# Attention of two token groups interleaved stage by stage, with the modulation vectors moved to other places

## The chip, the cores and the metric

The kernel runs on one core of one Trainium2 chip. The metric is the device time of one execution in microseconds (us). The kernel before was timed three times: 1448.36, 1448.42 and 1449.55 us, median 1448.42.

A core has engines that each work through their own list of instructions in order: PE (TensorE, matmuls into the PSUM banks), DVE (VectorE), ACT (ScalarE), POOL (GpSimd) and SP (SyncE, which here only issues DMAs). They wait for one another through semaphores. A DMA moves data from memory into the core while the engines work.

## The reference

Two layers of a transformer trunk, for two groups of 128 tokens with 1024 channels: context tokens (the prompt, group 0) and latent tokens (the sample, group 1). Per layer and group:

```python
h = adaln(rmsnorm(y, g_pre_mix[li]), m[0], m[1])        # m: six vectors per group
qa, ka, va, qb, kb, vb, up = split_projection(h @ w_in[li])     # 1024 -> 2560 columns
o_a = rmsnorm(diff_attention(qa, ka, va, lam), g_diff[li]) * (1.0 - lam_init)
o_b = dense_attention(qb, kb, vb)                       # sample: neighbourhood attention
o_c = multiscale_pool(up, pool_w[li], pool_scale[li])
y = y + m[2] * rmsnorm(merge_heads(o_a, o_b, o_c, w_out[li]), g_post_mix[li])
h = adaln(rmsnorm(y, g_pre_ffn[li]), m[3], m[4])
f = moe_ffn(h, ...)                                     # 64 experts, 8 per token, and a shared one
y = y + m[5] * rmsnorm(f, g_post_ffn[li])
```

The vectors are `m = silu(c) @ w_ada[li] + b_ada[li]`, cut into six of 1024; the prompt has its own `c`. Differential attention makes two softmaxes per head (four heads) and subtracts one, scaled by lambda, from the other. The sample's queries and keys are rotated first, and it also reads 128 cached context keys and values, so its scores have 256 columns where the prompt's have 128. All is fp32; the keys and values of the prompt are outputs too.

## The kernel before, in words

All is one program with the order written out by hand. Each layer has these stages.

*In-projection.* Tokens are normalised, transposed and modulated; the matrix `w_in` comes in five blocks of 512 columns. A projection is done as a split product (`split_product`, L651): activations and weights are cut into a high and a low part, and three products are added (high x high, low x high, high x low), 48 matmuls a block for both groups. The high part of a weight block is a copy by ACT (`high_weights`, L962), the low part a subtraction by DVE (`low_weights`, L1109). ACT copies the result of group 0, DVE that of group 1, into `U`. POOL rotates the sample's queries and keys (L482 to L487), after the last block.

*Attention.* `attention(l, 0)` runs whole, then `attention(l, 1)`: transposes of queries and keys (L535), scores (L546, or L549 and L550), exponentials on ACT (L984), combination of the two softmaxes on DVE (L1193), transposes of the weights (L585), values (L594), the same for the other heads (L564 to L610), and the pooling (L554, L579). The second call waits for the first to finish (`cat_done`), since both use the same buffers (`qkT`, `probs`, `wT`) and banks.

*Out-projection.* The concatenated heads are transposed (L515) and multiplied by `w_out` in two blocks; the vectors are spread over the partitions (L623).

*Experts.* Router, shared expert and the routed experts in pairs, in a loop. It takes most of the time, and the change does not touch it.

*Vectors.* The twelve vectors (six per layer, both groups at once) are made one at a time: `modulate` is 64 matmuls of 128x256 (L673) over two weight blocks, into a given PSUM bank, and `finish_vector` (L1122, L1126) adds the bias on DVE. If the bank was used for an earlier vector, PE first waits for that one's finish. Two vectors are made ahead of layer 0; in layer 0's attention five more (two of them in a row) and three in layer 1's; one behind each out-projection.

*Weight ring.* All weights ahead of the experts go through a ring of six blocks of 2 MB, in the order of the list from `blocks_before_experts`. SP issues block k when block k - 6 is done. An entry `("hi", ...)` is the place of a high part, which is not loaded; `("spare", k)` is an empty place. SP handles the list strictly in order, so a load whose place is not free holds up all behind it.

Line numbers here and in the rows are those of the kernel before.

## Time and profile before

| | |
|---|---|
| Three runs | 1448.36, 1448.42, 1449.55 us |
| The profiled execution | 1448.93 us, its span 1447.1 us |
| PE busy | 1357.5 us, 94% of the span |
| DVE, ACT, POOL busy | 466.7, 334.9, 60.3 us |
| Stages of layer 0 | in-projection 41.1 to 99.1, attention to 152.3, out-projection to 185.4 |
| Stages of layer 1 | in-projection 747.4 to 805.5, attention to 856.0, out-projection to 889.9 |

The span is what the profiler recorded of one execution, from its first to its last instruction. A busy PE is one with a matmul under way; its clock can still be at the lower of two levels (1.2 and 2.4 GHz), which the rows show as a granted clock of 0.50 against 1.00. The stages were cut by the first and last matmul of their kind.

### The profile page before, as it was taken

How to read it: one execution, taken by the hardware profiler on the slowest of the kernel's cores; microseconds unless marked ns; L12 is line 12 of the kernel's file. 1: busy time of each engine (PE TensorE's matmuls, PEld its weight loads, DVE VectorE, ACT ScalarE, POOL GpSimd, SP SyncE). 2: the span in 40 equal slices, each digit the busy share in tenths (PEclk: the TensorE clock that was granted, in tenths of full speed). 3: DMA queues.
4: the chain of work that ended last, by engine and by line, in shares of the span. 5: the costliest groups of instructions: out<-in, count | busy, mean ns of one | idle time of the engine just before them, and what ended most of it. 6: DMA issues, size and time to landing. Idle time of an engine off the chain costs nothing.

```text
span 1447.1 us, 30291 instructions
## 1 busy us (share of the span) xinstructions
PE 1357.5 (94%) x12298; PEld 744.4 (51%) x12298; DVE 466.7 (32%) x1110; ACT 334.9 (23%) x598; POOL 60.3 (4%) x89
## 2 busy tenths in 40 slices
PE   3898989999999999999969788999999999999996
PEld 2775744544544544544548575454454454454443
DVE  0625473222222222222264264622222222222223
ACT  1523441111111111111143344211111111111111
POOL 0120020000000000000020202000000000000000
PEclk8898989999999999999979978999999999999998
DMA  9789368999999999999656936399999999999990
GB/s 368 260 317 401 126 262 324 389 399 415 402 403 407 407 394 419 398 402 413 235 204 232 369 118 262 160 365 405 417 395 406 418 391 400 414 407 390 416 400 38
DMA packets 86294, 497.42 MB, mean 344 GB/s; under 512 B 7728, under 2 KB 7728, under 8 KB 36336
## 3 DMA queue, kind: packets, MB, share of 16 engines
q1 hardware_dynamic: 84416, 491.58, 84.7%
q0 software_dynamic: 1840, 5.31, 1.1%
q8 instruction: 27, 0.44, 0.1%
q14 instruction: 11, 0.09, 0.0%
HBM read 494.24 MB, written 2.62 MB: 343 GB/s over the span
## 4 chain that ended last, share of the span: by engine, by line
PE 88%; DVE 4%; ACT 3%; DMA 1%; issue 1%; SPq 1%; POOL 1%; POOLq 0%; ACTq 0%
PE PS L856 30%; PE PS L887 16%; PE PS L831 12%; PE PS L651 11%; PE PS L848 9%; PE PS L673 1%; PE PS L799 1%; DMA weights<-in_w_in 1%; PE PS L875 1%; PE PS L820 1%; SPq L384 1%; DVE h L1168 1%; PE PS L594 1%; PE PS L838 1%; ACT h L969 1%
## 5 line engine op out<-in xcount | busy, mean ns | idle before, releaser
L856 PE MATMUL PS<-weights,gathered 128*32 128x512 f32 (+1 forms) x3968 | 451.3, 592 | 0.0
L856 PEld LDWEIGHTS PS<-weights,gathered 128*32 128x32 f32 (+1 forms) x3968 | 133.6, 111 | 306.3 <-issue 306.3
L887 PE MATMUL PS<-weights,hiddenT 128*32 128x512 f32 (+1 forms) x1984 | 233.0, 595 | 0.0
L831 PEld LDWEIGHTS PS<-pick,x_parts 128*128 128x128 bf16 x3168 | 177.2, 98 | 54.7 <-issue 54.7
L831 PE MATMUL PS<-pick,x_parts 128*128 128x128 bf16 x3168 | 188.3, 219 | 0.0
L1473 DVE SCALAR_TENSOR_TENSOR hidden<-PS,slot_gate,silu 128x256 f32<-128x256 f32 x64 | 31.0, 484 | 397.8 <-ACT silu L1058 397.8
L1065 ACT ACTIVATE y_hi<-PS 128x512 fp32r<-128x512 f32 x128 | 76.4, 597 | 297.3 <-PE PS L887 297.3
L1483 DVE TENSOR_TENSOR y_lo<-PS,y_hi 128x512 fp32r<-128x512 f32 x128 | 88.5, 692 | 140.1 <-ACT y_hi L1065 140.1
L1058 ACT ACTIVATE silu<-PS 128x256 f32<-128x256 f32 x64 | 24.5, 383 | 417.5 <-PE PS L856 417.5
L887 PEld LDWEIGHTS PS<-weights,hiddenT 128*32 128x32 f32 (+1 forms) x1984 | 60.5, 110 | 116.0 <-issue 114.6
L651 PE MATMUL PS<-weights_split,hT_high 128*128 128x512 f32 x448 | 112.3, 407 | 7.8 <-ACT hT_high L943 6.0
L651 PEld LDWEIGHTS PS<-weights_split,hT_high 128*128 128x128 f32 x448 | 86.9, 196 | 30.4 <-issue 11.5
L848 PE MATMUL PS<-y_hi,put 128*128 128x512 f32 x264 | 88.4, 416 | 2.9 <-DVE y_lo L1483 2.9
L848 PE MATMUL PS<-y_lo,put 128*128 128x512 f32 x264 | 82.8, 395 | 0.0
L1476 DVE COPY gathered<-PS 128x512 f32<-128x512 f32 x64 | 44.3, 692 | 118.9 <-PE PS L831 118.9
L1109 DVE TENSOR_TENSOR weights_split<-weights,weights_split 128x4096 fp32r<-128x4096 f32 x14 | 61.6, 4421 | 9.8 <-ACT weights_split L962 9.8
L1439 DVE CAST put<-PS 128x256 fp32r<-128x256 bf16 x66 | 28.0, 424 | 103.9 <-PE PS L840 103.9
L437 POOL TENSOR_SCALAR rstd<-sum_squares 128x1 f32<-128x1 f32 x16 | 8.4, 528 | 1165.4 <-ACT h L969 1157.5
L673 PE MATMUL PS<-weights,c_columns 128*32 128x256 f32 x768 | 47.0, 399 | 9.5 <-DMA weights<-in_w_ada 9.5
L848 PEld LDWEIGHTS PS<-y_lo,put 128*128 128x128 f32 x264 | 49.5, 188 | 11.9
L651 PE MATMUL PS<-weights_split,hT_low 128*128 128x512 f32 x224 | 54.5, 395 | 0.0
L1060 ACT ACTIVATE gathered<-PS 128x512 f32<-128x512 f32 x64 | 38.2, 597 | 66.2 <-PE PS L831 66.2
(250 smaller groups left out, 983.5 us busy)
## 6 DMA issues: line engine op xcount, KB each, us to landing
weights<-in_w_gate SPq DMA_DIRECT2D x128, 1024.0 KB, 7.6
weights<-in_w_up SPq DMA_DIRECT2D x128, 1024.0 KB, 11.6
weights<-in_w_down SPq DMA_DIRECT2D x128, 1024.0 KB, 9.0
weights<-in_w_ada SPq DMA_DIRECT2D x24, 2048.0 KB, 13.1
weights<-in_w_in SPq DMA_DIRECT2D x9, 2048.0 KB, 8.3
weights<-in_w_out SPq DMA_DIRECT2D x4, 2048.0 KB, 15.9
weights<-in_w_in SPq DMA_DIRECT2D x2, 1024.0 KB, 24.1
weights<-in_ws_gate SPq DMA_DIRECT2D x2, 1024.0 KB, 5.1
```

What stands on the lines that cost most here:

```text
L651: last = mm(PS[:, banks[g], :], rows_[:, j, g, :], w[:, j * HALF:(j + 1) * HALF], start=start and j == 0, stop=w is lo and j == KT - 1, sk ...
L673: last = mm(PS[32 * q:32 * q + 32, bank, 0:QUARTER], cb[:, jj, :, :].rearrange("p g c -> p (g c)"), w[:, j, q * QUARTER:(q + 1) * QUARTER] ...
L831: last = mm(PS[:, 5 + half, j * P:(j + 1) * P], x3[:, g, part, jj, :], pick[:, u % 2, g, 0:P], start=(g, part) == (0, 0), stop=(g, part) = ...
L848: last = mm(PS[:, 2 * g + n, :], put[:, u % 2, g * T:(g + 1) * T], y[:, n * HALF:(n + 1) * HALF], start=False, stop=False, skip_group_chec ...
L856: last = mm(PS[a:z, 4, :].rearrange("p (a n) -> p a n", a=2), xgT[:, b, j, a:z], w[:, e, :, j, :], start=j == 0, stop=j == KT - 1, tile_po ...
L887: last = mm(PS[a:z, bank, :], hidT[:, j, a:z], w[:, e, j, n * HALF:(n + 1) * HALF], start=j == 0, stop=j == FT - 1, tile_position=(0, a), ...
L1060: run(*gathered(1 - b, 0), ACT.Copy).then_inc(S["xg_a"], 1)
L1065: run(yhi[:, n * HALF:(n + 1) * HALF], PS[:, bank, :], ACT.Copy).then_inc(S["yhi_done"], 1)
L1109: v.tensor_tensor(lo, w, hi.bitcast(f32), ALU.subtract).then_inc(w_low, 1)
L1473: v.scalar_tensor_tensor(hid[:, :], PS[:, 4, F:2 * F], slot_gate[:, b:b + 1], silu[:, :], ALU.mult, ALU.mult)\
L1476: v.tensor_copy(xgT[:, 1 - b, 4:8, :], PS[:, 6, :].rearrange("p (j s) -> p j s", j=4)).then_inc(S["xg_d"], 1)
L1483: v.tensor_tensor(ylo[:, cols], PS[:, bank, :], yhi[:, cols].bitcast(f32), ALU.subtract).then_inc(S["ylo_done"], 1)
```

## The change

Both groups now go through attention together: `attention(l)` on PE, ACT and DVE alternates between the groups, stage by stage. To that end each group has its own buffers (`qkT`, probabilities, transposed weights, pooled rows, row sums and maxima), laid over memory that is not in use at the time, and its own PSUM banks. The cache transposes go ahead of the last in-projection block, and POOL's rotation may start after the second block (its scratch is `h` and no longer `probs`). The in-projection uses four banks in turn (6, 7 and 4, 5).

The vectors are placed by new tables: in layer 0 one each behind in-projection blocks 1, 2 and 3 (all in bank 0), two within the scores, one behind the out-projection. In layer 1 vector (1, 2) is made ahead of the layer, before PE waits for the residual (`resid`), two are within the scores and one behind the out-projection.

```diff
-NEXT_LAYER = 2
-ADA_IN_ATTENTION = (((2, 1), (1, 1)), ((2, 0), (1, 0)))
-ADA_AFTER_OUT = (1, 1)
+AFTER_BLOCK = ({1: (0, 2), 2: (0, 3), 3: (0, 4)}, {})
+FIRST_VECTOR = (None, (1, 2))
+IN_SCORES = (((0, 5), (1, 0)), ((1, 3), (1, 4)))
+AFTER_OUT = ((1, 1), (1, 5))
...
 def blocks_before_experts(layer):
...
+    out = [b for i in range(EARLY) for b in halves((0, i))] if layer == 0 else halves(FIRST_VECTOR[layer])
+    for n in range(5):
+        out += [("in", n), ("hi", "in", n)] + halves(AFTER_BLOCK[layer].get(n))
+    for vector in IN_SCORES[layer]:
+        out += halves(vector)
+    for n in range(2):
+        out += [("out", n), ("hi", "out", n)]
+    spare = [("spare", k) for k in range(0 if layer else 1)]
+    return out + halves(AFTER_OUT[layer]) + spare + [("shared_gu",), ("shared_dn",)]
...
 # PE, in-projection
                 if l:
+                    modulate(FIRST_VECTOR[l], 5)
                     pe.wait_ge(resid, 2 * NG * l)
...
                 for n in range(5):
...
+                    if n > 1:
+                        pe.wait_ge(u_a, 5 * l + n - 1)
+                        pe.wait_ge(u_d, 5 * l + n - 1)
+                    split_product(l, "in", n, 3 * l, [6 - 2 * (n % 2) + g for g in range(NG)], u_mm)
+                    if n in AFTER_BLOCK[l]:
+                        modulate(AFTER_BLOCK[l][n], 0)
+                    if n == 3:
+                        pe.wait_ge(small_in, 128 * (l + 1))
...
-                attention(l, 0)
-                attention(l, 1)
+                attention(l)
 # PE, attention
+                heads_out(0, range(8), 0, 0)
+                pe.wait_ge(rope_done, l + 1)
+                pe.wait_ge(ct_ready, l + 1)
+                heads_out(1, range(8), 2, 0)
...
+                scores(0)
+                scores(1)
...
+                modulate(IN_SCORES[l][0], 4)
+                pe.wait_ge(sd_exp, NG * l + 1)
+                other_scores(0)
+                modulate(IN_SCORES[l][1], 5)
...
+                weights_out(0, 0)
...
+                other_scores(1)
+                values(0, 0)
+                pe.wait_ge(pt_ready, l + 1)
+                other_weights_out(0, 3)
...
+                weights_out(1, 1)
+                values(1, 2)
+                other_values(0, 3)
+                other_weights_out(1, 4)
+                other_values(1, 4)
 # DVE, in-projection
                 if l:
                     scaled_rows(4 * l)
+                    finish_vector(5)
...
                 for n in range(5):
                     if n < 4:
                         low_weights(l, "in", n + 1)
...
+                    if n - 1 in AFTER_BLOCK[l]:
+                        finish_vector(0)
                     dve.wait_ge(u_mm, 10 * l + 2 * n + 2)
```

SP in layer 0, from the second in-projection block on. `u_mm` is a finished projection block, `ada_mm` a finished half of a vector. Before:

```order
L390 DMA weights<-in_w_in 128x8x512 [waits block_in3,ada_mm]
L390 DMA weights<-in_w_in 128x8x512 [waits ada_mm]
L390 DMA weights<-in_w_in 128x8x512 [waits u_mm] x2
L390 DMA weights<-in_w_ada 128x4x1024 [waits u_mm] x6
L390 DMA weights<-in_w_ada 128x4x1024 [waits ada_mm] x4
L390 DMA weights<-in_w_out 128x8x512 [waits ada_mm] x2
```

And in the changed kernel:

```order
L394 DMA weights<-in_w_in 128x8x512 [waits block_in3,ada_mm]
L394 DMA weights<-in_w_ada 128x4x1024 [waits ada_mm] x2
L394 DMA weights<-in_w_in 128x8x512 [waits u_mm]
L394 DMA weights<-in_w_ada 128x4x1024 [waits u_mm] x2
L394 DMA weights<-in_w_in 128x8x512 [waits ada_mm]
L394 DMA weights<-in_w_ada 128x4x1024 [waits u_mm] x2
L394 DMA weights<-in_w_in 128x8x512 [waits ada_mm]
L394 DMA weights<-in_w_ada 128x4x1024 [waits u_mm] x2
L394 DMA weights<-in_w_ada 128x4x1024 [waits ada_mm] x2
```

The loads of the vectors now stand between those of the projection, and the fourth and fifth projection blocks (the first two that wait for `ada_mm` alone) wait for a vector's first half.

DVE in layer 0's in-projection, from the copy of block 1's result on: the subtraction for block 3 (`weights_split`), the lambda steps, and in the changed kernel the finish of a vector (`mod_raw`) between them and the next copy. Before:

```order
L1288 COPY U<-PS 128x512 [waits u_mm]
L1109 TENSOR_TENSOR weights_split<-weights,weights_split 128x4096 [waits w_high]
L1247 TENSOR_TENSOR lambda_rows<-lambda_rows 128x2x64 [waits lam_in]
L1247 TENSOR_TENSOR lambda_rows<-lambda_rows 128x2x64
L1251 TENSOR_REDUCE minus_lambda<-lambda_rows 128x2 [waits dve_step]
L1251 TENSOR_REDUCE minus_lambda<-lambda_rows 128x2
L1288 COPY U<-PS 128x512 [waits u_mm]
L1109 TENSOR_TENSOR weights_split<-weights,weights_split 128x4096 [waits w_high]
```

And in the changed kernel:

```order
L1355 COPY U<-PS 128x512 [waits u_mm]
L1154 TENSOR_TENSOR weights_split<-weights,weights_split 128x4096 [waits w_high]
L1311 TENSOR_TENSOR lambda_rows<-lambda_rows 128x2x64 [waits lam_in]
L1311 TENSOR_TENSOR lambda_rows<-lambda_rows 128x2x64
L1315 TENSOR_REDUCE minus_lambda<-lambda_rows 128x2 [waits dve_step]
L1315 TENSOR_REDUCE minus_lambda<-lambda_rows 128x2
L1167 TENSOR_TENSOR mod_raw<-PS,bias_and_gain 128x256 [waits ada_mm,vec_in]
L1171 SCALAR_TENSOR_TENSOR mod_raw<-mod_raw,bias_and_gain 128x256 [waits dve_step]
L1355 COPY U<-PS 128x512 [waits u_mm]
L1154 TENSOR_TENSOR weights_split<-weights,weights_split 128x4096 [waits w_high]
L1167 TENSOR_TENSOR mod_raw<-PS,bias_and_gain 128x256 [waits ada_mm,vec_in]
```

The finishes stand behind the subtraction of a later block.

PE in layer 0, from the first transposes (before) or the first vector of the scores (changed) on; `c_columns` is a vector, `U,probs` and `wT_prompt` are values, `na_` marks the other heads. Before, the prompt's group alone:

```order
L535 MATMUL PS<-const,U 128x128 x12
L546 MATMUL PS<-qkT 128x128 x8
L554 MATMUL PS<-const,U 64x128 x4
L564 MATMUL PS<-qkT 128x128 x4
L673 MATMUL PS<-weights,c_columns 32x256 x64
L579 MATMUL PS<-pool_w,cache_nk 128x64 x4
L585 MATMUL PS<-const,U 128x128 x4
L594 MATMUL PS<-U,probs 128x128 x4
L673 MATMUL PS<-weights,c_columns 32x256 x32
L599 MATMUL PS<-const,probs 128x128 x4
L610 MATMUL PS<-U,probs 128x64 x4
L535 MATMUL PS<-const,U 128x128 x12
```

And in the changed kernel, with both groups; first up to the sample's other scores, which go on for four more such rows:

```order
L701 MATMUL PS<-weights,c_columns 32x256 x32
L554 MATMUL PS<-qkT 128x128 x4
L701 MATMUL PS<-weights,c_columns 32x256 x32
L562 MATMUL PS<-const,U 128x128 x4
L621 MATMUL PS<-const,U 64x128 x8
L554 MATMUL PS<-qkT_sample 128x128
L556 MATMUL PS<-cacheT,qkT_sample 128x128
L554 MATMUL PS<-qkT_sample 128x128
L556 MATMUL PS<-cacheT,qkT_sample 128x128
```

And from the prompt's values to the sample's:

```order
L572 MATMUL PS<-U,wT_prompt 128x128 x4
L579 MATMUL PS<-const,na_probs_prompt 128x128 x4
L633 MATMUL PS<-pool_w,cache_nk 128x64 x4
L633 MATMUL PS<-pool_w,pooledT_sample 128x64 x4
L562 MATMUL PS<-const,U 128x128 x8
L572 MATMUL PS<-U,wT_sample 128x128
```

The prompt's values and other weights now lie between the sample's scores and its weight transposes.

## Rows read from the trace of the kernel before

**Rows 1.** The page: PE's granted clock in 40 slices of the span, in tenths.

```profile
PEclk8898989999999999999979978999999999999998
```

**Rows 2.** Busy time by stage: us, engines busy (instructions), granted clock, DMA share, GB/s.

```profile
41.10:99.10 58.00, 57.96 (x240) 46.75 (x240) 28.62 (x22) 20.82 (x17) 2.80 (x5) 0.95 0.73 271
99.10:152.30 53.20, 42.38 (x526) 30.91 (x527) 24.73 (x60) 19.41 (x63) 11.61 (x11) 0.90 0.97 368
152.30:185.40 33.10, 31.95 (x226) 23.46 (x225) 12.91 (x9) 15.24 (x22) 1.59 (x4) 1.00 0.24 87
805.50:856.00 50.50, 38.22 (x398) 30.37 (x399) 23.31 (x57) 21.27 (x64) 11.61 (x11) 0.83 0.74 278
856.00:889.90 33.90, 33.27 (x226) 24.84 (x225) 13.00 (x9) 14.88 (x22) 1.60 (x4) 0.96 0.31 117
```

**Rows 3.** PE in layer 0, by time (start, length), then a group: vectors in attention.

```profile
31.22 3.64 PE L673 MATMUL PS<-weights,c_columns 128*32 128x256 f32 x32 [3.91 <-DMA weights<-in_w_ada]
41.10 6.39 PE L651 MATMUL PS<-weights_split,hT_high 128*128 128x512 f32 x16 [4.04 <-ACT hT_high L943]
62.11 7.47 PE L651 MATMUL PS<-weights_split,hT_high 128*128 128x512 f32 x32
95.23 3.83 PE L651 MATMUL PS<-weights_split,hT_high 128*128 128x512 f32 x16
134.59 0.50 PE L564 MATMUL PS<-qkT 64*128 64x128 f32 x4 [2.19 <-ACT probs L984]
152.30 1.92 PE L515 MATMUL PS<-const,h 128*128 128x128 f32 x16
L673 PE MATMUL PS<-weights,c_columns 128*32 128x256 f32 x320 | 18.5, 387 | 0.0
```

**Rows 4.** PE by time, layer 1.

```profile
740.16 1.12 PE L632 MATMUL PS<-const,mod_raw 128*128 128x128 f32 x4 [7.28 <-DVE x L1170]
747.37 6.52 PE L651 MATMUL PS<-weights_split,hT_high 128*128 128x512 f32 x16 [2.01 <-ACT hT_high L943]
801.61 3.83 PE L651 MATMUL PS<-weights_split,hT_high 128*128 128x512 f32 x16
856.03 3.27 PE L515 MATMUL PS<-const,h 128*128 128x128 f32 x16
```

**Rows 5.** DMA from 720.5 to 742 in 40 slices; one load alone, issued 66.

```profile
GB/s 0 0 80 160 362 408 412 408 412 404 404 385 385 393 381 385 404 373 385 400 373 389 396 381 385 400 385 381 392 400 373 385 373 130 38 23 23 0 0 0
weights<-in_w_in SPq DMA_DIRECT2D x1, 2048.0 KB, 7.8
```

**Rows 6.** ACT and DVE by time: splits of weights, lambda, a vector's finish.

```profile
64.66 3.62 ACT L962 ACTIVATE weights_split<-weights 128x4096 fp32r<-128x4096 f32 x1
741.20 3.60 ACT L962 ACTIVATE weights_split<-weights 128x4096 fp32r<-128x4096 f32 x1
68.31 4.43 DVE L1109 TENSOR_TENSOR weights_split<-weights,weights_split 128x4096 fp32r<-128x4096 f32 x1 [1.64 <-ACT weights_split L962]
73.17 0.48 DVE L1251 TENSOR_REDUCE minus_lambda<-lambda_rows 128x2 f32<-128x128 f32 x2
120.60 0.42 DVE L1122 TENSOR_TENSOR mod_raw<-PS,bias_and_gain 128x256 f32<-128x256 f32 x1 [1.94 <-PE PS L673]
121.06 0.42 DVE L1126 SCALAR_TENSOR_TENSOR mod_raw<-mod_raw,bias_and_gain 128x256 f32<-128x256 f32 x1
```

**Rows 7.** Stretches of 2 us in which the clock changes.

```profile
46.00:48.00 2.00, 2.00 (x9) 1.62 (x8) 2.00 (x1) 0.89 (x1) 0.00 (x0) 0.89 1.07 360
134.00:136.00 2.00, 1.41 (x17) 1.41 (x19) 1.36 (x6) 0.54 (x3) 0.00 (x0) 0.80 1.03 392
144.00:146.00 2.00, 2.00 (x23) 1.08 (x26) 0.72 (x2) 0.60 (x1) 0.00 (x0) 0.64 0.64 238
752.00:754.00 2.00, 2.00 (x8) 1.56 (x8) 2.00 (x1) 1.16 (x1) 0.00 (x0) 0.75 0.00 0
```

**Rows 8.** POOL by time: a step of the norms beside a DVE instruction.

```profile
739.02 1.17 POOL L437 TENSOR_SCALAR rstd<-sum_squares 128x1 f32<-128x1 f32 x1 [2.99 <-ACT h L969]
```

More of the change, by code:

```diff
@@ new lines, in attention, with heads_out, scores, other_scores @@
+            def attention(l):
+                def heads_out(g, ks, bank, at):
+                    for k in ks:
+                        a = at + (k % 8) * P
+                        last = nc.tensor.transpose(PS[:, bank + k // 4 % 2, (k % 4) * P:(k % 4 + 1) * P], U[:, g, a:a + P], ident)
+                    last.then_inc(qk_mm, 1)
+                def scores(g):
+                    K, q = T * (1 + g), qkT[g]
+                    pe.wait_ge(qk_a, 3 * l + g + 1)
+                    pe.wait_ge(qk_d, 3 * l + g + 1)
+                    if g:
+                        pe.wait_ge(ct_ready, l + 1)
+                    for hh in range(DA_H):
+                        for m in range(2):
+                            r0 = 64 * m
+                            bank, col = (2 * m + hh // 2, (hh % 2) * K) if g else (6 + m, hh * K)
+                            last = mm(PS[:, bank, col:col + T], q[r0:r0 + 64, hh, :], q[r0:r0 + 64, 4 + hh, :], start=True, stop=True)
+                            if g:
+                                last = mm(PS[:, bank, col + T:col + K], q[r0:r0 + 64, hh, :], cacheT[r0:r0 + 64, hh, :], start=True, stop=True)
+                    last.then_inc(sd_mm, 1)
+                def other_scores(g):
+                    K, q, bank = T * (1 + g), qkT[g], (6, 4)[g]
@@ new lines, in values @@
+                def values(g, bank):
+                    nb = 1 + g
+                    pe.wait_ge(wt_a, NG * l + g + 1)
+                    for hh in range(DA_H):
+                        for b in range(nb):
+                            v = cdv[:, hh * DA_V:(hh + 1) * DA_V] if b else U[:, g, 2 * DA_W + hh * DA_V:2 * DA_W + (hh + 1) * DA_V]
+                            last = mm(PS[:, bank, hh * DA_V:(hh + 1) * DA_V], wT[g][:, hh * nb + b, :], v, start=b == 0, stop=b == nb - 1)
+                    last.then_inc(pv_mm, 1)
@@ new lines, in attention @@
+                last.then_inc(pt_mm, 1)
+                pe.wait_ge(mod_ready, started[0])
+                other_scores(1)
+                values(0, 0)
+                pe.wait_ge(pt_ready, l + 1)
+                other_weights_out(0, 3)
+                for g in range(NG):
+                    for w in range(4):
+                        r0, col = 64 * (w % 2), g * 2 * POOL_CH + (w // 2) * POOL_CH
+                        last = mm(PS[:, 6 + w % 2, col:col + POOL_CH], pooledT[g][r0:r0 + 64, w // 2, :],
+                                  poolw[r0:r0 + 64, w // 2, :], start=True, stop=True)
@@ L656, in split_product, with modulate @@
                         after(rows_ is hTlo, w is lo)
-            pending = [ada_order(l) for l in range(DEPTH)]
             started = [0]
             last_in = {}
-            def modulate(halves, bank):
+            def modulate(vector, bank):
                 if bank in last_in:
@@ L667, in modulate @@
                 last_in[bank] = started[0]
-                for what in halves:
+                for what in halves(vector):
                     w = use_block(pe, None, what).rearrange("p (j n) -> p j n", n=D)
@@ L676, in modulate @@
                     last.then_inc(ada_mm, 1)
-            def modulation(l, n, banks):
-                for k in range(n):
-                    modulate([pending[l].pop(0) for _ in range(2)], banks[k])
             pe.wait_ge(c_cols, 1)
@@ L735, in _ @@
                 pe.wait_ge(bcast, BCAST * (4 * l + 3))
-                modulation(l, ADA_AFTER_OUT[l], (7,))
-                assert not pending[l]
+                modulate(AFTER_OUT[l], 7)
                 pe.wait_ge(resid, NG * (2 * l + 1))
@@ L1277, in _ @@
                     scaled_rows(4 * l)
+                    finish_vector(5)
                 modulated_rows(l)
```

436 lines of the change are left out of this document (213 added, 223 removed).

## The prediction, made before the result was known

> **What bounds the kernel now.** I read the page first: TensorE (PE) is busy nearly all of the span, and the slices where its clock is below full lie at the start and around slice 20 [rows 1]. They are the two stretches ahead of the experts. Then I cut the trace by stage [rows 2]. In-projection of layer 0 (41.1 to 99.1 us) is solid PE work. Attention of layer 0 takes 53.2 us with PE busy 42.4, of layer 1 50.5 us with 38.2; there ACT is busy 19.4 and 21.3 and DVE 24.7 and 23.3, so no engine is full: the two groups go one after the other through a chain of short steps, and part of it runs at half clock (mean 0.90 and 0.83). The experts are not touched by the edit. Third, the order of PE in time gives the marks of each layer: one in-projection block is (95.23 - 62.11)/3 = 11.04 us, layer 0's projection ends at 95.23 + 3.83 = 99.06, the second block at 65.94, and the transposes of the concatenated heads start at 152.30 [rows 3]. In layer 1 the projection ends at 805.44, those transposes start at 856.03, and PE idles 7.28 us ahead of the layer [rows 4].
>
> **Sum, against the profiled execution.** Its time is 1448.93 us (span 1447.1); the median of the three runs is 1448.42, so the two can be taken for one another.
>
> *Layer 0, in-projection.* A vector is 64 matmuls and costs 18.5/5 = 3.7 us of PE at full clock [rows 3]. Three of them (0,2), (0,3), (0,4) move from the attention to behind blocks 1, 2 and 3. PE work is only moved; what matters is the weight ring, six blocks of 2 MB. The order of SP in the changed kernel puts the two loads of the next vector ahead of the next projection block, and that block's load now waits for the first half of the vector before it. So, with block 1 done at 65.94:
> - PE: vector (0,2) to 69.6, block 2 to 80.7. Block 2's own weights were asked for at 54.9 and land 7.8 us later [rows 5], in time.
> - SP: both halves of (0,3) leave at 65.94 and block 3 at about 67.8, behind them. Three such loads (6.3 MB) asked for together at 720.5 move from about 722.5 to 738.5, so the last lands 18.0 us after its issue [rows 5]. Block 3 lands at 83.9.
> - ACT's split takes 3.6 us (87.6), DVE's subtraction 4.4 (92.0) [rows 6].
> - The order of DVE puts `finish_vector` of (0,2) behind this subtraction and behind the lambda steps (two pairs of about 0.5, 1.0 us): 93.0, and its two instructions of 0.42 make 93.9 [rows 6].
> - PE's vector (0,3) uses the same bank 0 and waits for that: it starts at 93.9, not 80.7. **A new wait of 13.2 us.** Behind it in PE's queue stand block 3 and all that follows.
>
> PE has then stood so long that its clock is down: it fell at about 135, when PE had stood 2.2 us [rows 3, 7], and after the start at 41.10 was at half for some 5.2 us [rows 3, 7]; that costs 2.6 us. The first half of (0,3) takes 3.6 us at half clock [rows 3], so it is done at 97.5 and only then block 4 is asked for: landing 105.3, split 108.9, low part 113.4, `finish_vector` of (0,3) 113.8. PE ends (0,3) at 100.2 and block 3 at 111.2 and waits again, 2.6 us. Vector (0,4) to 117.5, the cache transposes (six of 0.12 with their start, 1.0) to 118.5, block 4 to 129.5. The projection ends 30.4 us later: 11.1 moved work, 1.0 of transposes that used to follow it, 13.2 + 2.6 waits, 2.6 clock.
>
> *Attention, either layer.* In the changed order PE has both groups' steps alternating, so that one group's ACT and DVE work lies beside the other's matmuls. What then ends last is PE. In layer 0 it was busy 42.4, less 18.5 for five vectors is 23.9 [rows 2, 3]; about 8 us of it ran at half clock between 135 and 145 [rows 7], so at full clock it is 19.7, less 1.0 for the cache transposes 18.7. With two vectors, 7.4, PE has 26.1. Following the new order I find two waits left that nothing fills: for ACT's copy of the sample weights (128x1024) before the values, and again for its twin before the last values, 1.1 each. Least: 28.3. If the half-clock share stays, 33.5. I take 30. ACT's 19.4 and DVE's 24.7 [rows 2] stay below that, and DVE loses three vector finishes.
> - Layer 0: 129.5 + 30 = 159.5 against 152.3: **+7.2**.
> - Layer 1 has no vectors inside the projection, so none of the waits above. From 805.44: 1.0 + 30 = 836.4 against 856.03: **-19.6**. Here 3.6 of it is the vector that leaves the attention.
>
> *Out-projection of layer 1.* It started at half clock: 33.9 us against 33.1 in layer 0 [rows 2]. With PE kept busy it should read as layer 0: **-0.8**.
>
> *Start of layer 1.* Vector (1,2) now lies in the wait of 7.28 us: its loads come first in the queue at 720.5, land at about 728 and 733, and PE does it from 732.9 to 736.6. The first projection block lands behind them at 738.5; ACT takes it up at 741.2 only [rows 6], so 2.7 us are left as cover. If that cover were gone, each us later would be a us of layer 1. DVE's extra 0.9 us stands ahead of the modulation columns, beside ACT's 3.6 us split, and is hidden too. The clock was at half until 753 [rows 7], and the first 16 matmuls took 6.52 [rows 4] where 16 of the last block took 3.83; the vector may save this (down to -2.5), or PE may sit still for 3.6 us after it as well and nothing changes. I take 0, the nearer row being the fall at 135 after a gap of 2.2 us.
>
> *Counted at nothing:* the rotation on POOL moves from after the last block to after the second. In layer 0 DVE stands idle there. In layer 1 it can hold up DVE's subtraction for block 3 (POOL and DVE do get in each other's way: a POOL step of 0.22 took 1.17 beside a DVE one [rows 8]); at most five steps, some 7.4 us, where PE wants the result 16 us after it can start. Three placeholder blocks fewer, and the shared weights asked for 12 us earlier, touch nothing that PE waited for.
>
> Sum: 7.2 - 19.6 - 0.8 = -13.2; 1448.93 - 13.2 = 1435.7, **forecast 1436 us**.
>
> **A page against the rows.** In layer 1's attention the granted clock was 0.83 on average although PE was busy 76% of it [rows 2]: half clock came in pieces, also between short matmuls. The Trainium skill (TensorE: Matmul & The Clock Gate, "What's actually happening") says that "the default state is throttled, and activity releases the throttle". By it the closer packed attention would stay at the upper level, 28.3 us and a time some 3 us below my forecast; by the row it may fall again, which is the second rival.
>
> **Rivals.**
> 1. *No new wait in the projection.* If block 3 came in time or DVE were not held, 13.2, 2.6 and 2.6 us go: 1436 - 18 = 1418. For it: in the stage as it was DMA had room, a busy share of 0.73 [rows 2]. Against: the order fixes both the load behind the vector and the finish behind the subtraction, and 18.0 us for three loads is a full-rate figure.
> 2. *The clock falls in the new attention as in the old.* A mean of 0.83 over 50.5 us is 17 us at half, worth 8.6 us; some 2 of them are in my 30. Another 6 in each layer: 1448, no change. For it: the steps after the second vector are short matmuls with waits, as then. Against: in layer 0 the first 35 us of attention, gaps and all, stayed at full clock until 135 [rows 7].
> 3. *Slower: the clock stays down after the 13 us wait.* From 93.9 PE has 3.7 + 11.0 + 3.7 + 1.0 + 11.0 = 30.4 us of full-rate work. At half clock to the end of the projection this costs 30.4, less the second wait and the 2.6 counted, 25: 1461. It decides from 16 us of this work at half (13.2 + 2.6). For it: from 26 to 46 us the clock was at half through vectors and the first block alike [rows 3]. Against: within solid block matmuls it came back after 5 us in layer 0 [rows 7] and by 753 in layer 1 [rows 7].
> 4. *The change gives nothing in attention:* if the chain inside one group, not the lack of the other's work, sets the time, attention stays near the sample group's 29 us plus the prompt's start, 36: 1448 again.
>
> **How the numbers follow.** Forecast 0.60, its own range 1429 to 1444 (attention 27 to 33 in each layer, the projection wait 10 to 16). Rival 1: 0.07. Rivals 2 and 4 together 0.19, reaching from 1442 to 1453. Rival 3: 0.10. Sundry losses that I don't see: 0.04. A measurement of this kernel tells about 0.2%, 3 us, from no change. Faster: 0.60 + 0.07 + 0.07 of the second group = 0.74. Same: 0.10. Slower: 0.02 + 0.10 + 0.04 = 0.16. Leaving most of rival 1 below and rival 3 above gives 1424 to 1452.
>
> **What would show it.** Right: in layer 0 PE waits some 13 us ahead of the second vector in the projection for DVE's `mod_raw`, and about 2.6 ahead of the third; block 3's weights land 18 us after their pair; a half-clock stretch follows; the projection ends near 129.5. Attention near 30 us in both layers, with PE busy over 85% and waits of about 1 us on ACT's wide copies. Layer 1 expert work starts about 20 us sooner counted from the layer's own start. Wrong: PE runs vector (0,3) at once; attention above 34 us; a wait for the first block's weights at the start of layer 1; the clock at half right up to 129.

## The result, and the profile after

The changed kernel took 1432.55 us (median of 1431.63, 1431.94, 1433.16 and 1435.14), the kernel before 1448.88 us beside it: a ratio of 0.989, 95% interval 0.9873 to 0.9907. That is 16 us faster; forecast were 1436 (1424 to 1452). Profiled was the execution of 1431.63 us, span 1429.8, 17.3 us below the span before.

The clock by slices answers [rows 1]. The two 7s of before (slices 21 and 24, from 724 and from 832 us: the start of layer 1 and its attention) are gone; slice 3 (71 to 107 us) is an 8 still, and holds the new wait in layer 0.

```profile
PEclk9889989999999999999999998999999999999999
```

The stages by the same view as [rows 2] (us, then PE, PEld, DVE, ACT, POOL busy, granted clock, DMA share, GB/s): in-projection, attention and out-projection of layer 0, then of layer 1.

```profile
41.00:131.40 90.40, 72.47 (x438) 53.74 (x439) 30.32 (x27) 21.72 (x19) 11.00 (x12) 0.89 0.80 307
131.40:159.40 28.00, 25.77 (x329) 20.78 (x328) 22.39 (x55) 17.93 (x59) 3.59 (x5) 1.00 0.95 365
159.40:193.10 33.70, 33.35 (x226) 25.00 (x225) 12.97 (x10) 15.55 (x22) 1.60 (x4) 0.95 0.23 86
754.40:811.70 57.30, 57.24 (x246) 46.79 (x247) 28.10 (x13) 20.30 (x17) 13.19 (x9) 0.98 0.69 253
811.70:839.70 28.00, 25.77 (x330) 20.75 (x328) 22.36 (x55) 19.19 (x60) 3.61 (x5) 1.00 0.93 342
839.70:873.00 33.30, 31.98 (x226) 23.53 (x225) 12.92 (x10) 15.46 (x22) 1.61 (x4) 1.00 0.32 119
```

Attention fell from 53.2 and 50.5 us to 28.0 in both layers, with PE busy 25.8 of it and the clock at the upper level throughout. Part of this is work that went elsewhere (three vectors in layer 0 and one in layer 1, 3.7 us each, and 1.0 us of cache transposes). Layer 0's in-projection, which took its part over, grew from 58.0 to 90.4 us, of which PE works 72.5. PE by time in that stage (answers to [rows 3]) shows the two new waits:

```profile
75.69 3.83 PE L680 MATMUL PS<-weights_split,hT_high 128*128 128x512 f32 x16
94.36 5.67 PE L701 MATMUL PS<-weights,c_columns 128*32 128x256 f32 x64 [14.83 <-DVE mod_raw L1171]
107.47 3.83 PE L680 MATMUL PS<-weights_split,hT_high 128*128 128x512 f32 x16
114.37 5.35 PE L701 MATMUL PS<-weights,c_columns 128*32 128x256 f32 x64 [3.07 <-DVE mod_raw L1167]
127.78 3.84 PE L680 MATMUL PS<-weights_split,hT_high 128*128 128x512 f32 x16
```

Behind block 2 (75.69, done at 79.5) vector (0,3) waits 14.83 us for the finish of (0,2), and (0,4) 3.07 us for that of (0,3). What DVE and ACT did meanwhile (answers to [rows 6]), and the loads that SP issued:

```profile
84.52 3.62 ACT L983 ACTIVATE weights_split<-weights 128x4096 fp32r<-128x4096 f32 x1 [18.27 <-DMA weights<-in_w_in]
88.17 4.43 DVE L1154 TENSOR_TENSOR weights_split<-weights,weights_split 128x4096 fp32r<-128x4096 f32 x1 [17.33 <-ACT weights_split L983]
93.04 0.48 DVE L1315 TENSOR_REDUCE minus_lambda<-lambda_rows 128x2 f32<-128x128 f32 x2
93.43 0.41 DVE L1167 TENSOR_TENSOR mod_raw<-PS,bias_and_gain 128x256 f32<-128x256 f32 x1
93.88 0.42 DVE L1171 SCALAR_TENSOR_TENSOR mod_raw<-mod_raw,bias_and_gain 128x256 f32<-128x256 f32 x1
64.70 0.92 SPq L394 DMA_DIRECT2D weights<-in_w_ada  x2
66.60 0.37 SPq L394 DMA_DIRECT2D weights<-in_w_in  x1
```

This is the chain to read: block 3's load leaves behind a pair of vector halves (64.70, 66.60), lands at 84.5, is split by ACT and then by DVE, and only behind that (and the lambda steps) stands the 0.8 us of DVE work for which PE has waited since 79.5. PE in layer 1 (answers to [rows 4]):

```profile
747.25 1.11 PE L661 MATMUL PS<-const,mod_raw 128*128 128x128 f32 x4 [3.19 <-DVE x L1215]
754.46 5.20 PE L680 MATMUL PS<-weights_split,hT_high 128*128 128x512 f32 x16 [2.01 <-ACT hT_high L964]
839.76 1.92 PE L519 MATMUL PS<-const,h 128*128 128x128 f32 x16
```

The wait ahead of the layer fell from 7.28 to 3.19 us since the vector fills it, but the layer's start did not come sooner for it: 747.25 is 7.1 us later than [rows 4] have it, as the end of layer 0's attention is. Inside layer 1's attention PE has just two waits:

```profile
PE PS L572 <- ACT wT_sample L1019: 1.1, 1, 1.1
PE PS L591 <- ACT na_wT_sample L1042: 1.1, 1, 1.1
```

The balance by marks: the end of layer 0's attention 159.43 against 152.30, +7.1; layer 1 from its first projection matmul to the end of attention 85.3 against 108.7, -23.4; its out-projection -0.6; experts and rest -0.4. Sum -17.3.

### The profile page after: what moved, and what is told of

Its sections match the earlier page's. It is cut to its first block, busy times and chain, and to the rows that moved or that the text cites. A ratio compares the mean times of both kernels' runs of the same rounds, so it can differ in the third digit from the quotient of the medians.

```text
span 1429.8 us, 30290 instructions
## 1 busy us (share of the span) xinstructions
PE 1344.9 (94%) x12298; PEld 734.1 (51%) x12298; DVE 466.5 (33%) x1110; ACT 334.3 (23%) x594; POOL 64.7 (5%) x89
## 4 chain that ended last, share of the span: by engine, by line
PE 88%; DMA 3%; DVE 3%; ACT 2%; issue 1%; SPq 1%; POOL 1%; ACTq 0%; POOLq 0%
PE PS L877 31%; PE PS L908 16%; PE PS L852 12%; PE PS L680 9%; PE PS L869 9%; DMA weights<-in_w_in 3%; PE PS L701 2%; PE PS L820 2%; PE PS L896 1%; PE PS L841 1%; ACT weights_split L983 1%; PE PS L772 1%; SPq L388 1%; DVE h L1213 1%; PE PS L859 1%
## 5 line engine op out<-in xcount | busy, mean ns | idle before, releaser
L680 PEld LDWEIGHTS PS<-weights_split,hT_high 128*128 128x128 f32 x448 | 85.3, 193 | 30.4 <-issue 12.3
L701 PE MATMUL PS<-weights,c_columns 128*32 128x256 f32 x768 | 50.8, 420 | 27.9 <-DVE mod_raw L1171 14.8
L983 ACT ACTIVATE weights_split<-weights 128x4096 fp32r<-128x4096 f32 (+1 forms) x14 | 49.1, 3508 | 46.0 <-DMA weights<-in_w_in 46.0
L869 PEld LDWEIGHTS PS<-y_lo,put 128*128 128x128 f32 x264 | 49.5, 188 | 10.7
```

The lines of the kernel that those rows point to most:

```text
L680: last = mm(PS[:, banks[g], :], rows_[:, j, g, :], w[:, j * HALF:(j + 1) * HALF], start=start and j == 0, stop=w is lo and j == KT - 1, sk ...
L701: last = mm(PS[32 * q:32 * q + 32, bank, 0:QUARTER], cb[:, jj, :, :].rearrange("p g c -> p (g c)"), w[:, j, q * QUARTER:(q + 1) * QUARTER] ...
L869: last = mm(PS[:, 2 * g + n, :], put[:, u % 2, g * T:(g + 1) * T], y[:, n * HALF:(n + 1) * HALF], start=False, stop=False, skip_group_chec ...
L983: run(hi, w, ACT.Copy).then_inc(w_high, 1)
```

## Experiments

The kernel before ran at medians of 1446.8 to 1448.7 us beside them. Times are medians.

**1. The finish of a vector ahead of the subtraction** (`e1_finish_first`).

```diff
                 for n in range(5):
+                    if n - 1 in AFTER_BLOCK[l]:
+                        finish_vector(0)
                     if n < 4:
                         low_weights(l, "in", n + 1)
...
-                    if n - 1 in AFTER_BLOCK[l]:
-                        finish_vector(0)
```

> The changed kernel, but on DVE the finish of a vector (bias added to mod_raw) stands ahead of the subtraction for the next projection block instead of behind it. Theory A (the 14.8 us wait for mod_raw ahead of the second vector in layer 0's in-projection comes from DVE's order together with the shared bank; the late landing of block 3's weights is a second limit behind it): the wait for mod_raw goes at both places; PE then waits about 5 us for block 3's high part, since its weights still land near 84 and the split is done near 88. Block 4 is asked for some 17 us sooner and makes PE wait no more. In-projection ends near 115 instead of 131.5, time 1416 us (1413 to 1420). Rival B (PE waits for the weights of block 3 in any case, the finish only stands beside it): the wait changes its name to the weights and stays near 14 us, time 1430 to 1433.

Measured 1418.18 us (1417.9 to 1419.1), ratio 0.9794. PE now makes vector (0,3) at once; what is left is a wait for block 3's weights themselves:

```profile
79.72 3.66 PE L701 MATMUL PS<-weights,c_columns 128*32 128x256 f32 x64
88.79 5.56 PE L680 MATMUL PS<-weights_split,hT_high 128*128 128x512 f32 x16 [5.41 <-ACT weights_split L983]
```

So the order of two pieces of DVE work costs this change 14 us.

**2. A second bank for the vectors** (`e2_two_banks`), DVE's order left as it is.

```diff
-                        modulate(AFTER_BLOCK[l][n], 0)
+                        modulate(AFTER_BLOCK[l][n], (n - 1) % 2)
...
-                        finish_vector(0)
+                        finish_vector((n - 2) % 2)
```

> The changed kernel with DVE's order as it is, but the vectors behind blocks 1, 2 and 3 go to banks 0, 1 and 0, so that the second does not wait for the first one's finish. Theory A: the late finish harms only through the shared bank, so this does the same as moving the finish: 1416 us (1413 to 1420), with DVE's finish of the first vector still near 94. Rival B: no change, 1430 to 1433. Rival C (the late finish also holds up something else, such as DVE's copies of the projection results into U): between the two, 1420 to 1428.

Measured 1414.78 us (1414.7 to 1419.5), ratio 0.9779. Here only the bank is different, so it is the shared bank through which the late finish reached PE; either cure removes the wait. Here too 5.49 us are left ahead of block 3, for its weights. The 3.4 us between the two cures are taken up in run 11.

**3. All three vectors behind the last block** (`p1_behind_last`), in banks 0, 1 and 2, their loads behind all of `w_in`.

```diff
-AFTER_BLOCK = ({1: (0, 2), 2: (0, 3), 3: (0, 4)}, {})
+AFTER_BLOCK = ({}, {})
+BEHIND = (((0, 2), (0, 3), (0, 4)), ())
```

> The changed kernel, but the three vectors (0,2), (0,3), (0,4) are made one after the other behind the last in-projection block, in banks 0, 1 and 2, and their loads stand behind those of the projection. Theory A (the interleaved attention is worth some 20 us by itself in either layer, and the spreading as it stands loses more than it brings): the in-projection is solid again to about 98; then DMA is the limit, since ten vector loads and two of w_out are drawn at 5.2 us each from 76 on; the three vectors end near 112, the attention waits for the weights of its two vectors for 5 to 8 us, layer 0's attention ends near 149 instead of 159.4: time 1422 us (1417 to 1430). Rival D (spreading is worth as much as its waits cost, because without it DMA holds up the attention by as much): 1430 to 1436.

Measured 1426.76 us (1422.0 to 1429.3), ratio 0.9857, the profiled run 1421.96. The blocks then run without a gap to 98.7, and so do (0,2) and (0,3) behind them. The third vector waits for the weights of both its halves, and so does the second of attention, 9.3 us in all:

```profile
109.25 3.61 PE L704 MATMUL PS<-weights,c_columns 128*32 128x256 f32 x32 [3.42 <-DMA weights<-in_w_ada]
130.13 3.41 PE L704 MATMUL PS<-weights,c_columns 128*32 128x256 f32 x32 [2.79 <-DMA weights<-in_w_ada]
```

This is faster than the changed kernel, but 9 to 12 us slower than the vectors between the blocks once their shared wait is gone (runs 1 and 2): between the blocks, their loads share the time of the projection.

**4. Are the vectors within the scores work that sets the length of attention?** (`m_short_vectors`)

```diff
-                modulate(IN_SCORES[l][0], 4)
+                modulate(IN_SCORES[l][0], 4, 1 if l else 4)
...
-                    for j in range(4):
+                    for j in range(steps):
```

> The changed kernel, but the two vectors within layer 1's scores do a quarter of their matmuls (a quarter of the sum over channels; the rest is left out), 1.8 us of PE work instead of 7.3. Theory P (as the prediction summed it: PE's work plus two waits sets the length of the new attention): layer 1's attention falls by 5.5 us to 22.5, time 1427 us. Theory Q (the vectors only fill the time in which ACT makes the exponentials; without them PE waits for these): it falls by the 1 to 1.5 us by which PE is behind the exponentials now, PE's wait for ACT takes the rest, time 1431 us (1430 to 1432).

Measured 1431.64 us, ratio 0.9889: no gain. Attention of layer 1 took 27.9 us, though PE was busy 22.0 us in place of 25.8 and its clock fell to 0.94 on average. Where the vectors' work went, PE waits for ACT's exponentials, and its short steps take longer afterwards (L562 1.11 us for 0.66):

```profile
809.90:837.80 27.90, 22.02 (x233) 18.81 (x232) 22.36 (x55) 19.20 (x60) 3.51 (x5) 0.94 0.91 346
818.24 0.71 PE L554 MATMUL PS<-qkT 64*128 64x128 f32 x8 [1.57 <-ACT probs_prompt L1004]
822.03 1.11 PE L562 MATMUL PS<-const,U 128*128 128x128 f32 x4 [2.08 <-ACT probs L1004]
```

ACT ended the exponentials 12.1 us after the end of the projection in both kernels. PE went on with L562 13.5 us after it in the changed kernel and 12.1 here, so of the 5.4 us taken out only 1.4 could come through, and the lower clock behind that took them back. In its first part attention is thus set by PE's work and ACT's almost alike, and the vectors there cost next to nothing.

**5. Without the vector in the wait ahead of layer 1** (`e5_vector_behind`): (1,2) is made behind the fifth block.

```diff
-AFTER_BLOCK = (..., {})
-FIRST_VECTOR = (None, (1, 2))
+AFTER_BLOCK = (..., {4: (1, 2)})
+FIRST_VECTOR = (None, None)
```

> The changed kernel with vector (1, 2) taken out of the wait ahead of layer 1 and made behind layer 1's fifth projection block instead (bank 0, its finish behind DVE's last copy). Theory A, as predicted: the vector is free in that wait, so it now costs its 3.7 us, and attention's first transposes wait for its finish, 1.1 us; the projection ends 3.7 later counted from its start. The start of layer 1 gives nothing back but DVE's 0.8 us finish. Time 1432.6 + 4 to 5 = 1437 (1435 to 1439). Theory B: the vector in the wait also keeps the clock up, and without it the projection starts at half for longer: 2 to 3 us on top, 1439 to 1440. Theory C: the vector's two loads ahead of the first block hold the layer up: the first block now starts sooner and the time is 1435 or less.

Measured 1437.33 us, ratio 0.9929: 4.8 us slower than the changed kernel. The wait ahead of the layer is 7.27 us again, the vector shows with its 3.7 us and its finish with 1.1:

```profile
745.92 1.11 PE L661 MATMUL PS<-const,mod_raw 128*128 128x128 f32 x4 [7.27 <-DVE x L1214]
812.00 3.66 PE L701 MATMUL PS<-weights,c_columns 128*32 128x256 f32 x64
816.76 2.84 PE L531 MATMUL PS<-const,U 128*128 128x128 f32 x24 [1.11 <-DVE mod_raw L1170]
```

Theory A gave the time; the vector in the wait is worth what it costs elsewhere.

**6. Layer 1's attention one group after the other again** (`e6_serial_layer1`), own buffers and the vectors' number kept.

```diff
 # PE, layer 1 (ACT and DVE in the same order)
+    scores(0)
+    modulate(IN_SCORES[l][0], 4)
+    other_scores(0)
+    modulate(IN_SCORES[l][1], 5)
...
+    other_values(0, 3)
+    pe.wait_ge(cat_done, NG * l + 1)
+    scores(1)
+    other_scores(1)
...
```

> The changed kernel with layer 1's attention (and only that) done one group after the other again on PE, ACT and DVE, with own buffers kept, both vectors in the prompt's part, and the same work in sum. Theory A: the alternation itself is what shortened attention. PE's 25.8 us of work are then joined by the sample's chain with nothing beside it; in the kernel before, attention of layer 1 took 50.5 us with PE busy 38.2, 3.7 of it a vector that is elsewhere now. I expect 50.5 - 3.7 - 1 for the cache transposes = 46, less up to 3 for a clock that stays higher: 42 to 46 in place of 28.0, and a time of 1447 to 1451. Theory B: own buffers and fewer vectors did it, and the alternation little: attention 28 to 33 and a time of 1432 to 1438.

Measured 1450.21 us (1448.0 to 1452.6, ten runs), ratio 1.0013. The same work now takes 46.4 us. PE is busy 32.5 us in it because its clock is 0.78 on average, and it waits 13.9 us; the waits over 1 us:

```profile
813.70:860.10 46.40, 32.52 (x330) 26.62 (x329) 22.68 (x55) 19.17 (x60) 3.55 (x5) 0.78 0.55 206
PE PS L554 <- ACT probs L1037: 6.4, 1, 6.4
PE PS L544 <- DVE h L1326: 2.1, 1, 2.1
PE PS L579 <- ACT na_probs_prompt L1045: 1.2, 1, 1.2
PE PS L562 <- DVE U L1306: 1.1, 1, 1.1
PE PS L572 <- ACT wT_sample L1052: 1.1, 1, 1.1
PE PS L591 <- ACT na_wT_sample L1076: 1.1, 1, 1.1
```

The alternation alone is worth 18 us in layer 1: 11.7 of waits (13.9 less the two of 1.1) and 6.7 of clock (PE busy 32.5 against 25.8). For layer 0 no run separates it.

**7 and 8. Another order of loads** on top of two banks. In `v1_load_order` blocks 3 and 4 are each asked for ahead of a pair of vector halves and (0,4) is made behind block 4; in `v2_split_pair` only block 3 moves, to between the two halves of (0,3).

```diff
 # v1_load_order
+AFTER_BLOCK   = ({1: ((0, 2), 0), 2: ((0, 3), 1), 4: ((0, 4), 5)}, {})
+LOADED_BEHIND = ({1: (0, 2), 3: (0, 3), 4: (0, 4)}, {})
 # v2_split_pair
+        if layer == 0 and n == 3:
+            first = out.pop()
+            out += block + [first] + vector
```

> The kernel with two banks for the vectors in layer 0's projection (1414.8) with another order of loads: projection block 3 is asked for ahead of the pair of vector (0, 3), block 4 ahead of the pair of (0, 4), and (0, 4) is made behind block 4 in bank 5. Theory A: each block then waits for nothing. The 5.5 us wait ahead of block 3 goes, at most 1 us comes for the second half of (0, 3) (issued at 68.3 behind two loads, landed at about 82 where PE wants it at 81.3); the projection with its three vectors ends at 111 in place of 116.6 and the time is 1410 (1408 to 1412). Theory B: the wait only moves to the loads of the two vectors in the scores, which now come in a row behind (0, 4): 3 us or more of waits for in_w_ada in attention, and a time of 1412 to 1415.

> The kernel with two banks (1414.8) with one place changed in the order of loads: projection block 3 of layer 0 is asked for between the two halves of vector (0, 3), not behind both. Theory A, the order of loads with the ring's free places sets what is left to wait: block 3 is the second of the loads asked for at 65 and lands near 78, its split is done at 82 and block 3 starts with no wait, where PE waited 5.5 us and then ran 1.4 us of its first matmuls at half clock; the second half of (0, 3) is asked for at 68 and lands near 83, a wait of 1 us; block 4's high part has to wait for block 3 to leave its place, some 2 us more. The four halves behind are asked for no later than before, so no wait in attention. Net -3 to -4 us: 1411 (1409 to 1413). Theory B, the DMA queue was full all along and any order gives the same sum, as the last try with whole blocks ahead of the pairs suggests: 1415 or more, the waits now standing ahead of block 4 or in attention.

Measured 1425.19 us (v1) and 1417.05 (v2), against 1414.78 and, in run 11, 1417.94 with two banks alone. Theory A failed in both. In v1 neither theory gave the time (B had 1412 to 1415). The wait ahead of block 3 went as meant, and the waits came where B had put them, at the vectors' own loads, but there were five of them with 10.7 us in sum, where B had 3 us or more. Four of the five are over 1 us; three of these:

```profile
85.23 1.93 PE L704 MATMUL PS<-weights,c_columns 128*32 128x256 f32 x32 [2.93 <-DMA weights<-in_w_ada]
125.11 3.29 PE L704 MATMUL PS<-weights,c_columns 128*32 128x256 f32 x32 [3.10 <-DMA weights<-in_w_ada]
135.34 3.29 PE L704 MATMUL PS<-weights,c_columns 128*32 128x256 f32 x32 [3.08 <-DMA weights<-in_w_ada]
```

In v2 the wait of 5.4 us ahead of block 3 became one of 3.4 ahead of the second half of (0,3), and the projection ended at 116.1 in place of 116.6. The time is theory B's (1415 or more), but not its waits: 0.2 us ahead of block 4, none for loads in attention. For v1 I take the ring as the reason, which no run tests: a block keeps its two places for as long as a whole block takes, and the loads of (0,4) left at 98.5, where they left at 79.6 with two banks alone.

**9 and 10. Is it the idle time ahead of layer 1 that lowers the clock?** Five matmuls of no use behind vector (1,2), in the changed kernel (`c1_keep_busy`) and with two banks (`v3_banks_busy`).

```diff
                     modulate(FIRST_VECTOR[l], 5)
+                    for _ in range(5):
+                        mm(PS[:, 6, 0:256], ident, C["band"][:, 0:256], start=True, stop=True)
```

> The changed kernel with five more matmuls of 128x256 (some 0.4 us each, their result unused) behind vector (1, 2) in the wait ahead of layer 1, so that PE stands about 1.1 us there in place of 3.2. Theory K: the idle time between that vector and layer 1's first transposes is what sends the clock to half. In the changed kernel the transposes (L661 1.11, L519 3.68) and the first 16 projection matmuls (5.20 in the profiled run, up to 6.7 in others) ran at half. With the clock kept up they read 0.66, 1.9 and about 4.2: 0.5 + 1.8 + 1 to 2.5 us less of PE time; but the transposes' end, not their length alone, leads on to the copies behind them, so 2.5 to 4.5 in all: 1432.6 - 3.5 = 1429 (1428 to 1430). Theory L: the clock does not hang on those 2 us (PE stands again, 2.0 us, ahead of the first projection matmuls): the rows stay at half and the time at 1432 to 1434.

> The kernel with two banks (1414.8, where the clock was already up at layer 1's first projection matmuls, 2.08 and 2.11 for the first 16) with the same five more matmuls. Theory K: the clock stays up through the transposes too (L519 3.48 becomes 1.9), 1 to 2 us: 1413 (1412.5 to 1414.5), and the runs lie closer together. Theory L: 1414.8, spread as before (1414.7 to 1419.5).

Measured 1431.39 and 1420.40 us (1416.7 to 1421.6): the first no more than 1 us from the changed kernel, the second no faster than two banks alone (1414.7 to 1419.8 in both series). In c1:

```profile
746.42 0.66 PE L661 MATMUL PS<-const,mod_raw 128*128 128x128 f32 x4 [1.29 <-DVE x L1217]
753.63 6.66 PE L680 MATMUL PS<-weights_split,hT_high 128*128 128x512 f32 x16 [3.08 <-ACT hT_high L966]
747.45 3.61 ACT L985 ACTIVATE weights_split<-weights 128x4096 fp32r<-128x4096 f32 x1
```

Half of theory K is right: with PE kept busy, the transposes run at the upper level (L661 0.66 us, where it was 1.11). But nothing comes of it. ACT's split of block 0's weights (747.45 to 751.1) stands ahead of the copies that PE needs, so PE merely waits 3.08 us in place of 2.01, in which the clock falls (0.50 from about 753 on), and the first projection matmuls start at the lower level again, 6.66 us. v3 shows the same (3.07 and 6.58 us). My sum counted PE's time and not ACT's behind it.

**11. Two banks once more** (`e2_again`).

> The kernel with two banks once more, unchanged. It differed by 3 to 4 us from the kernel with the earlier finish (1414.8 against 1418.2), though both take the same wait away. Theory R: the difference is how long TensorE stays at half clock at its first matmuls of a stage, which varies from execution to execution; then this median lies between 1414 and 1420 and its runs spread over 4 us or more. Theory S: two banks are really 3 us better: 1414.8 again within 1.

Measured 1417.94 us (1416.4 to 1419.8), theory R. The first 16 projection matmuls of layer 1 make 1.9 of the 3.1 us between the two profiled runs; first here, then in run 2:

```profile
738.98 6.39 PE L680 MATMUL PS<-weights_split,hT_high 128*128 128x512 f32 x16 [2.20 <-ACT hT_high L964]
```

```profile
738.60 2.08 PE L680 MATMUL PS<-weights_split,hT_high 128*128 128x512 f32 x8 [2.20 <-ACT hT_high L964]
740.94 2.11 PE L680 MATMUL PS<-weights_split,hT_high 128*128 128x512 f32 x8 [0.26 <-ACT hT_high L964]
```

The same instructions after the same wait of 2.20 us ran at half clock in the one and at full clock in the other. The wait did not decide it; the clock had fallen before it, in both runs, while PE transposed. Two stretches of 2 us, here (fall at about 734) and in run 2 (fall at about 733):

```profile
734.00:736.00 2.00, 1.75 (x10) 1.36 (x9) 1.92 (x6) 2.00 (x1) 1.73 (x4) 0.52 1.06 389
738.00:740.00 2.00, 1.02 (x3) 0.85 (x4) 1.53 (x4) 2.00 (x6) 1.89 (x4) 0.50 1.04 400
```

```profile
734.00:736.00 2.00, 2.00 (x11) 1.69 (x9) 1.93 (x7) 2.00 (x2) 2.00 (x4) 0.50 1.05 385
738.00:740.00 2.00, 1.40 (x6) 1.21 (x7) 1.31 (x3) 2.00 (x6) 1.50 (x3) 1.00 1.03 399
```

Cut finer, the clock of run 2 was back at about 737, ahead of the matmuls, and here only at about 744, in the midst of them. So runs 1, 2, 8 and 11 (1418.2, 1414.8, 1417.1, 1417.9) can't be told apart, and the cures of runs 1 and 2 are worth the same within 3 us.

**12. Layer 1 begun otherwise** (`v4_split_ahead`), on top of two banks: block 0 is loaded ahead of the vector, and ACT splits it ahead of the norms.

```diff
+        if layer and n == 0:
+            out += halves(FIRST_VECTOR[layer])
...
 # ACT
+                    high_weights(l, "in", 0)
                     norm_squares(lambda g: x[:, g, :], resid, NG * (2 * l - 1))
 # DVE
                 modulated_rows(l)
+                if l:
+                    finish_vector(5)
```

> The kernel with two banks, with layer 1 begun otherwise: projection block 0 is loaded ahead of vector (1, 2), ACT splits it ahead of the norms, and DVE finishes the vector behind the modulated rows. As the kernel with the five more matmuls showed, ACT's split of 3.6 us, not the transposes, stands last ahead of layer 1's first projection matmuls. Theory A: with the split out of the way these start when the transposes and the modulation columns are done, 1.0 to 1.5 us sooner; the vector's second half lands at about 730 and may cost 0.3. Time 1 us below the same call's run of the kernel with two banks (0.5 to 1.5, if the clock draws are alike; with them 0 to 4). Theory B: the vector's later loads hold PE up by more than that: equal or slower.

Measured 1419.14 us (1418.4 to 1422.1) beside 1417.94 in run 11: theory B, equal or slower. The vector's second half now lands last and holds PE up:

```profile
733.20 3.42 PE L703 MATMUL PS<-weights,c_columns 128*32 128x256 f32 x32 [4.37 <-DMA weights<-in_w_ada]
736.56 0.66 PE L663 MATMUL PS<-const,mod_raw 128*128 128x128 f32 x4
```

The columns are transposed at 736.56, where two banks alone had 731.4 to 731.8. The best version stays the changed kernel with two banks, or with the earlier finish: 1415 to 1418 us, 2.1% below the kernel before.

## Why the prediction was right, by its steps

*The wait in layer 0's projection* was forecast at 13.2 us, for DVE's finish of (0,2) behind the subtraction for block 3, and was 14.8. Each link stood where the prediction put it: loads at 64.7 (65.94 forecast), landed 84.5 (83.9), subtraction done 92.6 (92.0), finish done 94.3 (93.9). The size was off since the three loads took 19.8 us from the first issue and not 18.0. Between 64.0 and 84.6 us 7.25 MB were moved, where the three are 6.3: the next pair was asked for at 79.6 and, by these bytes, was under way before block 3 had landed, which my row of three loads alone could not show. That all of it came 1.3 us sooner than forecast (the first 16 matmuls took 5.26 us, where [rows 3] have 6.39) moved the loads and PE alike and is not in the wait. Runs 1 and 2 show the cause: take the order or the shared bank away and the wait is gone. The second wait was 3.1 us for 2.6. The clock fell in both waits (5.67 and 5.35 us for a vector of 3.7). That cost 2.0 and 1.7 us; the sum had 2.6 behind the first wait and nothing behind the second. So the projection ended at 131.5, not 129.5: 1.6 + 0.5 from the waits, 1.1 from the clock, less 1.3 from the earlier start. The granted clock around the long wait:

```profile
96.00:98.00 2.00, 2.00 (x24) 0.98 (x20) 0.00 (x0) 0.00 (x0) 0.00 (x0) 0.50 0.00 0
98.00:100.00 2.00, 2.00 (x34) 0.84 (x25) 0.00 (x0) 0.00 (x0) 0.00 (x0) 0.88 0.32 60
100.00:102.00 2.00, 2.00 (x13) 1.66 (x10) 0.00 (x0) 0.00 (x0) 0.00 (x0) 1.00 0.97 375
```

It was back at the upper level (2.4 GHz) at about 98.5, some 4 us after PE had started. That answers rival 3 (1461), which had it down to the end of the projection.

*Attention* was forecast at 30 us a layer, least 28.3, and was 28.0 in both. PE's 26.1 us of work (25.8 measured) and the two waits of 1.1 on ACT's wide copies are the rows above; what I added, 1.7 us for some clock at half, did not come. The clock was 1.00 through both, where [rows 2] had 0.90 and 0.83. Rival 2 (the clock falls as before) is out. Run 6 shows for layer 1 that the alternation does it and nothing else in the change, against rival 4: one group after the other took 46.4 us, near the 45.9 of before without its third vector and the cache transposes. The rule that the prediction quotes from the Trainium skill (TensorE: Matmul & The Clock Gate, "What's actually happening"), that activity releases the throttle, gave 28.3 for this stage, and the trace agrees (28.0 us at a granted clock of 1.00). One thing of this step was wrong though the number was right: I had PE alone setting the length. By run 4 the first part of attention is ACT's exponentials nearly as much, and the two vectors there are all but free. Their 7.4 us are in my sum of PE's work; with 5.4 of them taken out, attention kept its length (27.9 us), and some 1.4 us is the most that it could have lost. That PE's sum and ACT's came out so close was luck.

*Layer 0 in sum* was forecast +7.2 and came out +7.1, from two errors of 2.0 us that cancel: the projection longer, attention shorter. That it came so close is luck.

*Layer 1's attention* was forecast -19.6, and here lies most of the 4.1 us by which the sum of -17.3 beats the -13.2 forecast. It went from 50.6 to 28.0 us and 1.0 of cache transposes, -21.6; the rest of the -23.4 is the first projection matmuls (5.20 us for 6.52, -1.3) and 0.5 of sundries.

*Start of layer 1*, forecast 0 with a bound of -2.5: -1.3 in the profiled run, but by run 11 this can be 2 us more or less without any cause in the kernel. That the vector costs nothing in the wait is shown by run 5.

*Out-projection of layer 1* -0.6 (-0.8). Experts and rest -0.4 (0). Layer 0's out-projection, counted at nothing, took 0.6 us more since it began at the lower level (33.7 us at 0.95, for 33.1 at 1.00), and its experts as much less. POOL's rotation, also counted at nothing, cost nothing: PE was busy 57.24 of the 57.30 us of layer 1's projection.

*Rival 1*, that there is no wait, was priced at 1418. It did not happen, but runs 1 and 2 take both waits away and land at 1418.2 and 1414.8. The nearness to 1418 is in part luck: 21.6 us of waits and clock went (14.8, 3.1 and 3.7), where the rival had 18, and 5.4 us of waiting for block 3, with 1.5 to 1.7 us of half clock behind it, came in their place.

Open is why the clock fell some 1 us sooner in run 2 than in run 11 and came back some 7 us sooner. And the 5.4 us that block 3 still waits in the best version: runs 7, 8 and 12 moved such waits and gained nothing.

## What to carry to other kernels

When work is interleaved to fill one engine, look at the small step by which a shared buffer or bank comes free, and at what is queued ahead of it on its engine: here 0.8 us of DVE work behind a 4.4 us subtraction and its load cost 14 us, where the alternation of both groups gave 18 in layer 1. In a ring with a strict order a load put first made another late (runs 7, 8 and 12), so a change of order is to be summed over all consumers, not for the one that waits. And a chain of short steps pays twice, in its waits and in the clock that falls in them (run 6: 11.7 and 6.7 us).

## What the runs showed of the hardware that I had not expected

- The wait just ahead does not tell the clock of a stage. After 2.20 us of waiting, the same matmuls ran at the upper level in one profiled run and at the lower in the other (2.08 and 2.11 us for twice 8 against 6.39 for 16); in both the clock had fallen before that wait, and in one it was back in time. At the start of layer 0 the first 16 took 5.24 to 6.70 us in the profiled runs. Small gains of 1 to 3 us can't be read from a median where a stage starts after a wait.
- ACT's copies of 128x1024 held PE up by 1.11 us in the profiles of the changed kernel and of all 12 runs, twice in either layer and whatever was changed around them, which makes such a wait a term that can be counted on here.
